# One decoder layer on one core: which queue begins which piece of the first loads

## The chip, the cores and the metric

The kernel runs on 1 NeuronCore of a Trainium2 chip. The metric is the device time of one execution in microseconds (us), as the median over runs; lower is better.

## The reference, cut to what matters

One layer of a decoder trunk on x of shape (1, 256, 1024) in float32: parallel token mixing (two attention branches that share one input projection), cross-attention into 256 memory tokens, a squared-ReLU MLP, and a last RMSNorm. The change touches only the first products, those of the normed input with the first columns of w_in:

```
h = rmsnorm(x, g_mix[l])
proj = h @ w_in[l]
qa = split_heads(proj[..., 0:MOBA_WIDTH], MOBA_HEADS)
```

The kernel multiplies x by the gain g_mix first and applies the row's rsqrt to the products later, so that the products can begin before the norm is known.

## The kernel before

All weights (some 76 MB) are streamed once from HBM in chunks of 128 partitions x 2048 float32 (1 MB). A float32 product is made of three products of halves: each operand is split into a high part (ScalarE, ACT: a copy that rounds to fp32r) and a low part (VectorE, DVE: the whole minus the high part), and TensorE (PE) adds high x high, low x high and high x low in PSUM.

**The head.** The first two chunks of w_in (chunk 0 and chunk 1, 256 output columns each) and the transposed x are not loaded as whole chunks but in nine pieces that lie one behind the other in the tensor `front`, in tile `head_all`. The contraction of 1024 has eight k-tiles of 128 rows:

- piece 0: x and chunk 0 for k-tile 0, and the gains (128 rows of 2176 bytes, 272 KB)
- piece 1: x and chunk 0 for k-tile 1 (128 rows of 2048 bytes, 256 KB)
- piece 2, the pair: chunk 1 for k-tiles 0 and 1 (256 KB)
- pieces 3 to 8, the triples: x, chunk 0 and chunk 1 for k-tiles 2 to 7 (128 rows of 3072 bytes, 384 KB each)

Behind them come four halves (512 KB each) of chunks 2 and 3, the two tiles of x by tokens (`res`), and whole chunks from 4 on.

**Who issues the loads.** Two engines' queues issue transfers: SyncE (SP) and ScalarE (ACT). The tuple `ACT_PIECES` names the pieces that ScalarE begins (line 469); all other pieces, the halves and everything after are SyncE's, in the order of their numbers (lines 346 to 361). Before the change ScalarE begins pieces 1 and 3, and then loads its table of functions (line 470, `preload_act_table_set`).

**What consumes them.** The order is written out by hand and is the same on the three engines: k-tile 0, k-tile 1, the pair, then k-tiles 2 to 7. For each k-tile ScalarE waits for the piece (`head_arrived`), makes `hT_hi` (line 494) and the high part of the weights (line 497; line 502 for the pair); VectorE makes `hT_lo` (line 761) and `w_lo` (line 732); TensorE does its products (line 1226 and its neighbours in `head_products`): 6 matmuls of 256 columns for k-tile 0, 6 for k-tile 1, 12 for the pair, 12 for each triple. Before all of that TensorE runs eight products of zeros (`WARM_UP`, line 1217), which the trace shows as 16 matmuls. Each engine works through its list in order. After the head TensorE goes on with chunks 2, 3, 4 ... (line 1168); a chunk's buffer is loaded again when TensorE has used it (`w_used`), so that later loads follow TensorE.

Of the kernel before, what the change touches and what calls it, by code (L numbers as in the profile page):

```python
# [57 lines left out]
def hybrid_layer(nc, x, front, mem, memT, g_final, weights, ff, out):  # L58
# [66 lines left out]
    FRONT = [2 * SEQ + GAINS, 2 * SEQ, 2 * SEQ] + (KT - FIRST) * [3 * SEQ] + 4 * [CH // 2]  # L125


    ACT_PIECES = (1, 3)

    def front_piece(j):  # L130

        begin = P * sum(FRONT[:j])
        return front[begin:begin + P * FRONT[j]].rearrange("(p n) -> p n", p=P)
# [3 lines left out]
    with ctx:  # L137
# [98 lines left out]
        def piece(j):  # L236

            ends = HEAD - 2 * SEQ * min(j, PAIR + 1) - 3 * SEQ * max(j - PAIR - 1, 0)
            return head_all[:, ends - (2 if j <= PAIR else 3) * SEQ:ends]
# [98 lines left out]
        def _(sp):  # L338
# [7 lines left out]
            for j in range(HEAD_PIECES):  # L346
                dst = piece(j) if j else head_all[:, HEAD - 2 * SEQ:HEAD + GAINS]
                if j not in ACT_PIECES:
                    sp.dma_start(dst, front_piece(j)).then_inc(head_arrived[j], 16)
# [115 lines left out]
        def _(act):  # L465
            copy = nc.scalar.activation

            for j in ACT_PIECES:
                act.dma_start(piece(j), front_piece(j)).then_inc(head_arrived[j], 16)
            nc.scalar.preload_act_table_set("natural_log_exp_and_others")  # L470

            def split_hi(slot, rslot, arrived, used):
                act.wait_ge(raw_in[rslot], arrived)
# [668 lines left out]
        def _(pe):  # L1142
# [77 lines left out]
            def head_products(tiles, n, last=False):  # L1220

                def products(wt, v, wait=None):
                    for c, k in tiles:
                        for m in range(2):
                            a = k * SEQ + m * P
                            i = mm(halves(c)[m], wt[:, c, a:a + P], v[:, k, :],  # L1226
                                   start=k == 0 and m == 0 and wt is w_hi and v is hT_hi,
                                   stop=last and wt is w_lo, skip_group_check=True)
                        if last and wt is w_lo:
                            i.then_inc(w_used, 1)  # L1230

                x_tiles = 1 + max(k for _, k in tiles)
                pe.wait_ge(hi_done[X], x_tiles)
                pe.wait_ge(*((w_hi_ready, 2) if last else (piece_hi, n)))
                products(w_hi, hT_hi)
                pe.wait_ge(lo_done[X], x_tiles)
                products(w_hi, hT_lo)
                pe.wait_ge(*((w_lo_ready, 2) if last else (piece_lo, n)))
                products(w_lo, hT_hi)
# [325 lines left out]
```

## Time and profile before

| what | value |
|---|---|
| median of 3 runs | 412.04 us (411.45 to 412.25) |
| the profiled execution | 412.37 us, span 410.5 us |
| PE busy | 401.8 us (98%) |
| DVE busy | 331.0 us (81%) |
| ACT busy | 251.2 us (61%) |
| HBM traffic | 188 GB/s over the span |

The span runs from the first to the last instruction; the rest of an execution's time lies outside it. All starts below are in us from the span's start. TensorE is busy for nearly the whole span, so what matters is when its work begins, whether it waits afterwards, and what comes after its last product.

### The profile page before, as it was taken

How to read it: one execution, taken by the hardware profiler on the slowest of the kernel's cores; microseconds unless marked ns; L12 is line 12 of the kernel's file. 1: busy time of each engine (PE TensorE's matmuls, PEld its weight loads, DVE VectorE, ACT ScalarE, POOL GpSimd, SP SyncE). 2: the span in 40 equal slices, each digit the busy share in tenths (PEclk: the TensorE clock that was granted, in tenths of full speed). 3: DMA queues.
4: the chain of work that ended last, by engine and by line, in shares of the span. 5: the costliest groups of instructions: out<-in, count | busy, mean ns of one | idle time of the engine just before them, and what ended most of it. 6: DMA issues, size and time to landing. Idle time of an engine off the chain costs nothing.

```text
span 410.5 us, 7028 instructions
## 1 busy us (share of the span) xinstructions
PE 401.8 (98%) x2857; PEld 370.5 (90%) x2857; DVE 331.0 (81%) x410; ACT 251.2 (61%) x298; POOL 27.8 (7%) x41
## 2 busy tenths in 40 slices
PE   8999999999999999999999999999999999999993
PEld 8999978999999999889998899899999999999982
DVE  5769566967755737874958888999999999999985
ACT  7664338864765634561556648777777777777764
POOL 0089000000000000000200000000000000000013
PEclk9999999999999999999999999999999999999998
DMA  8999554534325255545454245455565555656002
GB/s 318 415 419 388 204 204 156 179 126 158 115 102 195 104 206 205 195 184 174 165 170 139 102 145 196 179 208 205 214 203 212 200 206 198 208 206 243 2 0 102
DMA packets 12395, 77.46 MB, mean 189 GB/s; under 512 B 1361, under 2 KB 1361, under 8 KB 4049
## 3 DMA queue, kind: packets, MB, share of 16 engines
q1 hardware_dynamic: 12080, 76.44, 50.6%
q10 hardware_dynamic: 288, 0.66, 0.4%
q8 instruction: 19, 0.31, 0.3%
q14 instruction: 8, 0.06, 0.0%
HBM read 76.04 MB, written 1.05 MB: 188 GB/s over the span
## 4 chain that ended last, share of the span: by engine, by line
PE 91%; DVE 3%; ACT 2%; issue 1%; DMA 1%; POOLq 0%; POOL 0%; DVEq 0%; ACTq 0%
PE bank L1168 36%; PE bank L1496 16%; PE bank L1193 16%; PE bank L1315 11%; PE bank L1226 3%; PE bank L1327 1%; PE bank L1513 1%; PE bank L1420 1%; DMA head_all<-in_front_dram 1%; PE bank L1440 1%; PE bank L1209 1%; PE bank L1368 1%; ACT hT_hi L484 1%; DVE w_lo L732 1%; DVE t_lo L732 1%
## 5 line engine op out<-in xcount | busy, mean ns | idle before, releaser
L732 DVE TENSOR_TENSOR w_lo<-raw,w_hi 128x2048 fp32r<-128x2048 f32 (+2 forms) x69 | 143.6, 2088 | 23.4 <-ACT w_hi L476 22.4
L1168 PE MATMUL bank<-hT_hi,w_hi 128*128 128x256 f32 (+1 forms) x369 | 102.2, 277 | 0.0
L1168 PE MATMUL bank<-hT_lo,w_hi 128*128 128x256 f32 x368 | 101.8, 277 | 0.0
L1168 PE MATMUL bank<-hT_hi,w_lo 128*128 128x256 f32 x368 | 101.7, 276 | 0.0
L476 ACT ACTIVATE w_hi<-raw 128x2048 fp32r<-128x2048 f32 x32 | 61.0, 1917 | 27.4 <-PE bank L1168 14.2
L1168 PEld LDWEIGHTS bank<-hT_hi,w_hi 128*128 128x128 f32 x369 | 69.3, 188 | 0.1
L1168 PEld LDWEIGHTS bank<-hT_lo,w_hi 128*128 128x128 f32 x368 | 69.2, 188 | 0.1
L1168 PEld LDWEIGHTS bank<-hT_hi,w_lo 128*128 128x128 f32 x368 | 69.1, 188 | 0.0
L1315 PE MATMUL bank<-hT_hi,w_hi 128*128 128x256 f32 x128 | 35.8, 279 | 0.0
L1315 PE MATMUL bank<-hT_lo,w_hi 128*128 128x256 f32 x128 | 35.4, 277 | 0.0
L1315 PE MATMUL bank<-hT_hi,w_lo 128*128 128x256 f32 x128 | 35.4, 277 | 0.0
L732 DVE TENSOR_TENSOR t_lo<-t_sum,t_hi 128x2048 fp32r<-128x2048 f32 x15 | 34.4, 2293 | 0.0
L662 ACT ACTIVATE f_hi<-forms 128x896 fp32r<-128x896 f32 (+1 forms) x16 | 15.2, 949 | 27.5 <-DVE forms L1041 26.9
L628 ACT ACTIVATE w_hi<-raw 128x2048 fp32r<-128x2048 f32 x16 | 30.3, 1903 | 0.0
L635 ACT ACTIVATE w_hi<-raw 128x1536 fp32r<-128x1536 f32 (+1 forms) x16 | 24.0, 1500 | 1.4 <-PE bank L1193 1.4
L1315 PEld LDWEIGHTS bank<-hT_hi,w_hi 128*128 128x128 f32 x128 | 24.1, 188 | 0.2 <-issue 0.2
L1315 PEld LDWEIGHTS bank<-hT_lo,w_hi 128*128 128x128 f32 x128 | 24.1, 188 | 0.1
L1315 PEld LDWEIGHTS bank<-hT_hi,w_lo 128*128 128x128 f32 x128 | 24.0, 188 | 0.0
L1496 PE MATMUL bank<-t_lo,f_hi 128*128 128x512 f32 x60 | 23.4, 390 | 0.0
L1496 PE MATMUL bank<-t_hi,f_hi 128*128 128x512 f32 x60 | 23.4, 389 | 0.0
L1496 PE MATMUL bank<-t_hi,f_lo 128*128 128x512 f32 x60 | 23.3, 389 | 0.0
L647 ACT ACTIVATE t_hi<-t_sum 128x1024 fp32r<-128x1024 f32 x15 | 15.9, 1061 | 9.7 <-DVE t_sum L981 9.7
(213 smaller groups left out, 875.0 us busy)
## 6 DMA issues: line engine op xcount, KB each, us to landing
raw<-in_weights_dram SPq DMA_DIRECT2D x64, 1024.0 KB, 4.8
raw<-in_front_dram SPq DMA_DIRECT2D x4, 512.0 KB, 9.2
head_all<-in_front_dram SPq DMA_DIRECT2D x5, 384.0 KB, 6.3
res<-in_x_dram SPq DMA_DIRECT2D x2, 512.0 KB, 12.9
mem_tok<-in_mem_dram SPq DMA_DIRECT2D x1, 1024.0 KB, 11.9
memT_raw<-in_memT_dram SPq DMA_DIRECT2D x1, 1024.0 KB, 10.8
gfin<-in_g_final_dram SPq DMA_DIRECT2D x1, 512.0 KB, 5.5
out_dram<-xs SPq DMA_DIRECT2D x2, 256.0 KB, 2.0
```

Of the source, the lines that this page charges most:

```text
L476: copy(w_hi[:, slot, :], raw[:, rslot, :], ACT.Copy).then_inc(w_hi_ready, 1)
L484: copy(dst[:, k, :], t_tile(n, k), ACT.Copy, scale=gT[:, g + k:g + k + 1]).then_inc(hi_done[n], 1)
L628: copy(w_hi[:, c % RING, :], raw[:, c % RAW, :], ACT.Copy).then_inc(up_hi, 1)
L635: copy(w_hi[:, c % RING, 0:cols], raw[:, c % RAW, 0:cols], ACT.Copy).then_inc(down_hi, 1)
L647: copy(t_hi[:, u % 2, 2 * H:4 * H], t_sum[:, u % 2, 2 * H:4 * H], ACT.Copy).then_inc(t24_hi, 1)
L662: copy(f_hi[:, u % 2, first:upto * P], forms[:, first:upto * P], ACT.Copy).then_inc(f_hi_done, 1)
L732: return nc.vector.tensor_tensor(dst, whole, high.bitcast(fp32), sub)
L1168: last = mm(outs[m][:, tok], w, v[:, k0 + k, tok], start=first and n == 0 and not t, stop=k == nk - 1 and n == 2, skip_group_check=bool(kt ...
L1193: last = mm(outs[t][c][:, a:e], s, w[:, a_ + a:a_ + e], start=start and k == 0 and n == 0, stop=stop and k == nk - 1 and n == 2, skip_grou ...
L1226: i = mm(halves(c)[m], wt[:, c, a:a + P], v[:, k, :], start=k == 0 and m == 0 and wt is w_hi and v is hT_hi, stop=last and wt is w_lo, ski ...
L1315: last = mm(halves(h % 2)[m], w, v[:, kk, :], start=kk == 0 and n == 0, stop=kk == KT - 1 and n == 2)
L1496: last = mm(bank[p][:, a:e], s, w[:, n * H + a:n * H + e], start=start and j == 0, stop=u == PAIRS - 2 and p in (P1, P6, P7) and j == 2, s ...
```

## The change

ScalarE loads its table first and then begins pieces 3, 5 and 7 (the triples of k-tiles 2, 4 and 6). SyncE begins pieces 0, 1, 2, 4, 6 and 8, and then, as before, the halves and the rest. What is loaded, where it goes, and what waits for it stay as they are.

```diff
-    ACT_PIECES = (1, 3)
+    ACT_PIECES = (3, 5, 7)
...
+            nc.scalar.preload_act_table_set("natural_log_exp_and_others")
             for j in ACT_PIECES:
                 act.dma_start(piece(j), front_piece(j)).then_inc(head_arrived[j], 16)
-            nc.scalar.preload_act_table_set("natural_log_exp_and_others")
```

## Rows read from the trace of the kernel before

**Rows 1.** Chain that ended last, in order of time (start, us, what).

```profile
0.73 0.07 issue
0.80 3.50 DMA head_all<-in_front_dram
4.30 0.02 issue
4.33 0.51 ACT hT_hi L494
4.84 0.32 ACT w_hi L497
5.15 0.14 issue
5.29 11.99 PE bank L1226 x96
...
398.17 5.48 PE bank L1513 x24
```

**Rows 2.** Waits of PE over the whole span (us in total, times, longest).

```profile
PE bank L1226 <- ACT w_hi L497: 0.4, 1, 0.4
PE bank L1496 <- DVE f_lo L732: 0.4, 1, 0.4
```

**Rows 3.** DMA issues of 1.1 to 1.3 and of the last head piece (issue to landing).

```profile
head_all<-in_front_dram ACTq DMA_DIRECT2D x1, 384.0 KB, 4.7
head_all<-in_front_dram SPq DMA_DIRECT2D x1, 272.0 KB, 3.5
head_all<-in_front_dram ACTq DMA_DIRECT2D x1, 256.0 KB, 3.7
head_all<-in_front_dram SPq DMA_DIRECT2D x1, 256.0 KB, 4.4
...
head_all<-in_front_dram SPq DMA_DIRECT2D x1, 384.0 KB, 7.2
```

**Rows 4.** Timeline of ACT's queue and engine, 0 to 7 (start, us).

```profile
0.80 0.89 ACTq L469 DMA_DIRECT2D head_all<-in_front_dram  x2
1.72 1.28 ACT L470 ACT_TABLE_LOAD   x1 [1.72 <-PEq L1555]
5.75 0.62 ACT L502 ACTIVATE w_hi<-head_all 128x512 fp32r<-128x512 f32 x1
6.28 0.49 ACT L494 ACTIVATE hT_hi<-head_all 128x256 fp32r<-128x256 f32 x1
6.67 0.62 ACT L497 ACTIVATE w_hi<-head_all 128x512 fp32r<-128x512 f32 x1
```

**Rows 5.** Timeline of PE, 1 to 9.

```profile
1.12 3.78 PE L1217 MATMUL bank<-zeros 128*128 128x128 f32 x16 [1.12 <-DVE zeros L785]
5.85 0.63 PE L1226 MATMUL bank<-hT_lo,w_hi 128*128 128x256 f32 x2
6.28 0.63 PE L1226 MATMUL bank<-hT_hi,w_lo 128*128 128x256 f32 x2
6.71 0.58 PE L1226 MATMUL bank<-hT_hi,w_hi 128*128 128x256 f32 x2
7.13 0.40 PE L1226 MATMUL bank<-hT_lo,w_hi 128*128 128x256 f32 x2
7.59 0.62 PE L1226 MATMUL bank<-hT_hi,w_hi 128*128 128x256 f32 x4
8.95 0.62 PE L1226 MATMUL bank<-hT_hi,w_hi 128*128 128x256 f32 x4
```

**Rows 6.** Packets by DMA queue, 2.5 to 3.5 (q1 is SyncE's, q10 ScalarE's).

```profile
q1 hardware_dynamic: 94, 0.20, 52.0%
q10 hardware_dynamic: 96, 0.19, 49.9%
```

**Rows 7.** Packets by DMA queue, 1.5 to 2, 2 to 2.25 and 2.25 to 2.5.

```profile
q1 hardware_dynamic: 11, 0.02, 41.0%
...
q1 hardware_dynamic: 16, 0.03, 99.4%
q10 hardware_dynamic: 2, 0.00, 4.3%
...
q1 hardware_dynamic: 10, 0.02, 29.9%
q10 hardware_dynamic: 11, 0.02, 26.1%
```

**Rows 8.** Stretch by stretch: busy time of each engine, granted PE clock, DMA share, GB/s.

```profile
3.00:3.25 0.25, 0.25 (x3) 0.25 (x3) 0.00 (x0) 0.01 (x1) 0.00 (x0) 1.00 1.09 405
3.25:3.50 0.25, 0.25 (x3) 0.25 (x3) 0.00 (x0) 0.00 (x0) 0.00 (x0) 1.00 1.02 395
```

**Rows 9.** Timeline of ACT around its second table load.

```profile
138.16 0.58 ACT L525 ACTIVATE aT_hi<-bank 128x512 fp32r<-128x512 f32 x1
138.75 1.28 ACT L578 ACT_TABLE_LOAD   x1
140.05 1.07 ACT L578 ACTIVATE gateT<-gateT 128x1024 f32<-128x1024 f32 x1
```

## The prediction

> **What bounds the kernel now.** I read the chain that ended last first. It begins with the first piece of the head: issued at 0.80, landed at 4.30, then ScalarE's two copies, then TensorE from 5.29 [rows 1]. From there the chain is TensorE almost to the end, and TensorE's own waits say the same: after its start it waits 0.4 us once, for the head, and 0.4 us once, in the MLP [rows 2]. Later loads follow TensorE's use of the buffers, so nothing between 5.29 and the last product at 398.17 is set by a clock of its own. So the time moves by as much as the head's products move, and by nothing else. The question is when each piece of the head lands, and whether TensorE is ready for it.
>
> In the timeline of TensorE the products of k-tile 0 start at 5.29, those of k-tile 1 at 6.71, of the pair at 7.59, of the triple of k-tile 2 at 8.95 [rows 1, 5]. Up to about 7.1 two matmuls of 256 columns take 0.43 us (5.85 to 6.28 to 6.71), 0.213 us each, which is 1.2 GHz; from 7.59 twelve take 1.36 us, 0.113 us each, near 2.4 GHz [rows 5]. The column of the granted clock reads 1.00 in this stretch as well [rows 8], so here the pace is the better witness. By 7.11 TensorE had worked from 1.12 on, with one pause before 5.29.
>
> ScalarE took the copies one behind the other without waiting: the pair's at 5.75, k-tile 2's at 6.28 and 6.67 [rows 4]. A triple costs ScalarE 0.92 us a step (0.39 + 0.53, from the starts), against 1.36 us on TensorE. After the pair TensorE is the slower one, and ScalarE gets ahead of it.
>
> **How the pieces share the DMA engines.** Pieces 0 and 1 were issued together at 0.80 and landed at 4.3 and 4.5; pieces 2 and 3 were issued at 1.24 and landed at 5.64 and 5.94 [rows 3, 4]. Between 2.5 and 3.5 SyncE's queue moved 94 packets and ScalarE's 96 [rows 6]: the two take turns packet by packet, at some 400 GB/s together [rows 8]. A packet is one row of a transfer, 2176 bytes in piece 0, 2048 in pieces 1 and 2, and 3072 in a triple. By 2.5 SyncE's queue had moved 11 + 16 + 10 = 37 packets [rows 7], so that the 91 that were left of piece 0 were through at about 3.5; it landed 0.8 us later. I take 0.8 us from last packet to landing for all.
>
> **The change, part by part.**
>
> *Where ScalarE's transfers begin.* This decides the sign. Either ScalarE's queue issues while the table load runs (issues from about 0.85), or it waits until that is over (from 0.80 + 1.28 = 2.08). No row shows a DMA issue behind a table load. The nearest rows are those of the second table load: it starts 0.01 us after the copy before it ended, and the next activation starts 0.02 us after it [rows 9]. It behaves like a link in the engine's own queue, with the next instruction already handed over, so that whatever hands instructions over did not stand still for the 1.28 us. A DMA issue is the work of that part (it is shown on ACTq, not on ACT, [rows 4]), and I take it that it runs on. The hint is weak, since a table load also starts 0.03 us after a DMA issue [rows 4], which is no longer a gap.
>
> The Trainium skill bears on this (Advanced Engine Details and Errata, Sequencer Loop): an engine instruction is pushed into the engine's queue, and others can be read meanwhile. By that rule the table load holds back no issue, and the sum would be the one below; no run here has shown it yet.
>
> *Piece 0.* Beside it now runs piece 3, with rows of 3072 instead of 2048 bytes. The 91 packets take 91 x (2176 + 3072) bytes = 478 kB, 1.19 us at 400 GB/s instead of 0.96 (91 x 4224): through at 3.7, landed at 4.5, 0.2 us late. TensorE starts 0.99 us after the landing (4.30 to 5.29, [rows 1]): 5.5.
>
> *Piece 1.* It now stands behind piece 0 in SyncE's queue, not beside it. For 128 rows of 2048 bytes beside rows of 3072 the trace has an example: piece 2 beside piece 3, from 3.5 to 5.64 - 0.8 = 4.84, 1.34 us [rows 3]. Strictly packet by packet it would be 128 x 5120 bytes = 655 kB, 1.64 us. I take the measured 1.34, and keep 1.64 as the bound: through at 5.04, landed at 5.84, 1.3 us later than now. Ready for TensorE at 5.84 + 0.99 = 6.83. TensorE is done with k-tile 0 at 5.5 + 1.42 = 6.92, so that this delay is covered, by 0.1 us. (At 1.64 it is 7.13, a wait of 0.2 us, which the next step swallows.)
>
> *Piece 2, the pair.* Another 1.34 us: through at 6.38, landed at 7.18, 1.5 us later than now. ScalarE's copy takes 0.62 us [rows 4], and 0.14 + 0.02 us of handing over [rows 1]: TensorE can start the pair at 7.18 + 0.8 = 7.98. It is done with k-tile 1 at about 7.65 (6 matmuls from 6.92, one or two at the slow pace). It waits 0.3 us, and the pair starts at 7.98 instead of 7.59: **+0.4 us**. With 1.64 us each for pieces 1 and 2: through at 3.7 + 3.28 = 6.98, landed at 7.78, pair at 8.58: +1.0 us.
>
> *The triples.* Pieces 3 and 5 come earlier than they are needed. Piece 4 (k-tile 3) is behind piece 2 in SyncE's queue, beside piece 7: at most 128 x 6144 bytes = 786 kB, 2.0 us: landed at 9.2. ScalarE's two copies (0.39 + 0.62) and the hand-over make 10.35; TensorE needs it at 7.98 + 2 x 1.36 = 10.7. Covered by 0.35 us. The bytes of all the pieces are the same, so the last one still lands at about 3.63 + 7.2 = 10.8 [rows 3] and is needed after 16. Nothing behind it is moved: halves, x and chunks 4 on follow in the same stream of bytes.
>
> *One issue fewer on SyncE, one more on ScalarE.* An issue takes 0.45 us (0.89 for two, [rows 4]). SyncE's list is 0.45 us shorter, which buys nothing: the stream behind the head runs on at full rate and is limited by bytes. ScalarE's three end at 2.2, or at 3.45 if held back; ScalarE idles until 4.3. Nothing else stands in its queue that anyone awaits. The table load itself is hidden before as after; uncovered it would cost 1.28 us.
>
> The sum is +0.4 us, against 412.37 us for the profiled execution and 412.04 us for the median. I put it on the median: **412.4 us**. What a measurement of this kernel can tell from no change is about 0.2%, 0.8 us.
>
> **The rivals.**
>
> *A. The table load holds the issues back.* Then nothing runs beside pieces 0 and 1 (ScalarE's first packets came 1.4 us after its issue, [rows 7]; now at 3.5). By 2.5 between 37 and all 50 packets of both queues are piece 0's; the other 78 to 91, at 2176 bytes each, take 0.42 to 0.50 us: landed at 3.7 to 3.8, TensorE ready at 4.7 to 4.8. The warm-up products cover this: sixteen from 1.12 at 0.22 us each end their turn at 4.7 [rows 5]. TensorE starts 0.5 to 0.6 us early. Piece 1 lands at 4.5 or before; the pair (by 3.65 + 1.64 + 0.8 = 6.1) is ready at 6.9, before TensorE wants it. If the pace still steps up at 7.1, the 2.6 matmuls gained are worth only 0.113 us each, 0.3 us; if it steps with the work, the whole 0.55. Time 411.5 to 411.7. For it: the release of the other queue is plain arithmetic. Against it: rows 9.
>
> Here the Trainium skill has a price of its own (ScalarE: Activation LUTs, What ACT_TABLE_LOAD costs): a drain of about 1.38 us beside the 1.28 us. With both, the issues would begin at about 3.5 and the triple of k-tile 2 would come about 0.1 us after TensorE wants it, an estimate from that page. The trace disagrees: activations start 0.02 us behind the load [rows 9].
>
> *B. The queues take turns strictly.* The end on the slow side: the 1.64 us bound holds for both pieces, and the pair starts at 8.58. Time 413.0. It decides once piece 2 lands later than 7.6 (pair at 8.4). For it: 94 to 96 packets [rows 6]. Against it: piece 2 took 1.34 us in the same company.
>
> *C. The queues share by bytes.* Then piece 0 isn't late, piece 1 is through at 3.5 + 541/400 = 4.85 and the pair's at 4.85 + 1.31 = 6.16, landed at 6.96, pair at 7.76: +0.2 us, 412.2, as good as no change. Against it: rows 6, though there the rows were of nearly one size.
>
> **How the numbers follow.** Forecast 0.47, A 0.28, B 0.15, C 0.10. Medians of three runs here lie 0.8 us apart at most, so I give each case about 0.4 us either way. Slower by over 0.2% (above 412.86): most of B and a tenth of the forecast, 0.17. Faster by over 0.2% (below 411.22): a fifth of A, 0.06. Within: 0.77. The range goes from A's lower end, 411.4, to B's value with a little of its spread, 413.1.
>
> **What the profile after would show.** ScalarE's three issues at about 0.85 to 2.2 (A: 2.1 to 3.45). Piece 0 landed at 4.5, piece 1 at 5.8, piece 2 at 7.2. TensorE's first product at 5.5, a wait of about 0.3 us before the pair's, the pair at 8.0; from there everything 0.4 us later than before, and no other new wait. The prediction is wrong if TensorE's first product comes before 5.2, if a triple is awaited, or if the step of the pace has moved by 1 us or more.

## The result and the profile after

The changed kernel takes **414.26 us** (median of 6 runs, 414.04 to 416.21) against 411.83 us before (median of 6). The ratio is **1.0068, 95% interval 1.0055 to 1.0082**: slower by about 2.4 us of the medians, where +0.4 us and 412.4 us were forecast, too little to be told from no change. It lies above the forecast range, which ended at 413.1 us.

The profiled execution took 414.14 us with a span of 412.2 us, 1.7 us more than the span before. The chain that ended last begins as follows (start, us, what); the rows of before are [rows 1]. The products are counted up to 13 us only.

```profile
0.80 3.94 DMA head_all<-in_front_dram
4.74 0.02 issue
4.76 0.51 ACT hT_hi L494
5.27 0.31 ACT w_hi L497
5.59 0.14 issue
5.72 3.16 PE bank L1226 x12
...
8.88 4.20 PE bank L1226 x32
```

The first piece lands 0.44 us later (4.74 instead of 4.30) and TensorE's first product comes 0.43 us later. The larger step comes behind it: the pair starts at 8.88 instead of 7.59 ([rows 5]). The timeline of ScalarE and its queue shows why, beside [rows 4].

```profile
0.79 1.28 ACT L468 ACT_TABLE_LOAD   x1 [0.79 <-PEq L1555]
0.82 1.36 ACTq L470 DMA_DIRECT2D head_all<-in_front_dram  x3
...
6.30 0.51 ACT L494 ACTIVATE hT_hi<-head_all 128x256 fp32r<-128x256 f32 x1 [0.72 <-DMA head_all<-in_front_dram]
...
8.11 0.63 ACT L502 ACTIVATE w_hi<-head_all 128x512 fp32r<-128x512 f32 x1 [1.00 <-DMA head_all<-in_front_dram]
8.65 0.49 ACT L494 ACTIVATE hT_hi<-head_all 128x256 fp32r<-128x256 f32 x1
```

The three issues begin at 0.82, while the table load runs from 0.79 to 2.07: it holds nothing back. ScalarE, which before went from copy to copy, now waits for piece 1 (until 6.3) and for the pair (until 8.1). SyncE issues pieces 0, 1 and 2 at 0.80, 1.24 and 1.71. The lines of the DMA issues give their landings (last column, us from issue to landing).

```profile
head_all<-in_front_dram ACTq DMA_DIRECT2D x1, 384.0 KB, 4.2
head_all<-in_front_dram SPq DMA_DIRECT2D x1, 272.0 KB, 3.9
...
head_all<-in_front_dram SPq DMA_DIRECT2D x1, 256.0 KB, 5.0
...
head_all<-in_front_dram SPq DMA_DIRECT2D x1, 256.0 KB, 6.4
```

Piece 0: 0.80 + 3.9 = 4.7. Piece 1: 1.24 + 5.0 = 6.2. Piece 2: 1.71 + 6.4 = 8.1, against 5.64 before [rows 3]. The timeline of TensorE around it:

```profile
7.82 0.63 PE L1226 MATMUL bank<-hT_lo,w_hi 128*128 128x256 f32 x2
8.25 0.63 PE L1226 MATMUL bank<-hT_hi,w_lo 128*128 128x256 f32 x2
8.88 1.02 PE L1226 MATMUL bank<-hT_hi,w_hi 128*128 128x256 f32 x4
9.74 0.62 PE L1226 MATMUL bank<-hT_lo,w_hi 128*128 128x256 f32 x4
```

In this execution the pace stays at 0.21 us a product up to about 9.5 (before: 7.1, [rows 5]), so that the pair's first four products take 0.86 us instead of 0.45. The 1.29 us at the pair become 1.70 us behind it, and 1.70 us is the difference of the spans. From k-tile 2 on this trace is that of before, shifted.

### The profile page after: what moved, and what is told of

Same layout as the page of the kernel before. It is cut to its first block, busy times and chain, and to the rows that moved or that the text cites. A ratio compares the mean times of both kernels' runs of the same rounds, so it can differ in the third digit from the quotient of the medians.

```text
span 412.2 us, 7028 instructions
## 1 busy us (share of the span) xinstructions
PE 403.0 (98%) x2857; PEld 371.3 (90%) x2857; DVE 330.5 (80%) x410; ACT 250.8 (61%) x298; POOL 28.0 (7%) x41
## 4 chain that ended last, share of the span: by engine, by line
PE 91%; DVE 3%; ACT 2%; issue 1%; DMA 1%; POOLq 0%; POOL 0%; DVEq 0%; ACTq 0%
PE bank L1168 36%; PE bank L1496 16%; PE bank L1193 16%; PE bank L1315 11%; PE bank L1226 3%; PE bank L1327 1%; PE bank L1513 1%; DMA head_all<-in_front_dram 1%; PE bank L1420 1%; PE bank L1440 1%; PE bank L1209 1%; PE bank L1368 1%; ACT hT_hi L484 1%; DVE t_lo L732 1%; DVE w_lo L732 1%
```

## The experiments

Each kernel was timed against the kernel before in the same rounds. The ratio is to that kernel, with its 95% interval. The start of the pair and the landing of piece 2 are from one profiled execution each (us).

| run | ScalarE's pieces | ratio (95%) | piece 2 lands | pair starts |
|---|---|---|---|---|
| before | 1, 3 | 1 | 5.6 | 7.6 |
| changed | 3, 5, 7 behind the table load | 1.0068 (1.0055 to 1.0082) | 8.1 | 8.9 |
| pieces_only | 3, 5, 7 ahead of it | 1.0055 (1.0041 to 1.0069) | 8.0 | 8.8 |
| table_only | 1, 3 behind it | 1.0008 (0.9996 to 1.0020) | 5.7 | 7.5 |
| sp_only | none | 1.0011 (1.0000 to 1.0022) | 5.3 | 6.3 |
| act1 | 1 | 1.0009 (0.9998 to 1.0019) | 5.2 | 7.0 |
| act12 | 1, 2 | 1.0007 (0.9990 to 1.0023) | 5.8 | 7.5 |
| act3 | 3 | 1.0040 (1.0025 to 1.0054) | 6.2 | 7.4 |
| act35 | 3, 5 | 1.0050 (1.0033 to 1.0067) | 7.3 | 8.7 |
| held | 3, 5, 7 after the table load is over | 1.0053 (1.0038 to 1.0067) | 7.6 (again: 5.4) | 8.4 (again: 6.8) |

**The two parts of the change, each alone.** First the split of the pieces without the move of the table load:

```diff
-    ACT_PIECES = (1, 3)
+    ACT_PIECES = (3, 5, 7)
```

> The changed kernel with the table load put back behind ScalarE's three issues, so that only the split of the pieces differs from before. Theory 1 (the triples in ScalarE's queue take three fifths of the bytes while pieces 0, 1 and 2 wait, and the table load has no part in it): as slow as the changed kernel, ratio 1.005 to 1.008; piece 2 lands at about 8.1 and the pair starts at 8.7 to 9.0. Theory 2 (the table load beside the first issues slows the first packets: 143 GB/s at 2.5 to 2.75 against 364 before): the first packets come as fast as before, piece 2 lands at about 7.2, ratio 1.001 to 1.003.

Then the move without the split (`ACT_PIECES = (1, 3)`, table load ahead of the issues):

```diff
+            nc.scalar.preload_act_table_set("natural_log_exp_and_others")
             for j in ACT_PIECES:
                 act.dma_start(piece(j), front_piece(j)).then_inc(head_arrived[j], 16)
-            nc.scalar.preload_act_table_set("natural_log_exp_and_others")
```

> The kernel before with its own pieces 1 and 3 in ScalarE's queue, but with the table load ahead of the issues. Theory 1: no change (0.998 to 1.002); piece 0 lands at 4.3 and the pair starts at 7.6. Theory 2: pieces 0 to 2 land 0.3 us or more later than before and the rate at 2.5 to 2.75 is near 143 GB/s; ratio 1.001 to 1.003.

The split alone gives the whole loss (1.0055, the interval overlaps that of the changed kernel), the move alone none (1.0008, interval across 1). Theory 2 falls: in table_only the rate at 2.5 to 2.75 was 298 GB/s (364 and 407 in the two profiles of before) and piece 0 landed at 4.0, earlier than in the first profile of before, while in pieces_only the rate was 209 GB/s with the table load out of the way. The slow first packets go with the triples; whether the table load takes a little of the rate too isn't shown, and it costs no time that can be told.

**What runs beside pieces 0 to 2: a ladder.** Only the tuple `ACT_PIECES` differs, and the table load stands behind the issues: `()`, `(1,)`, `(3,)`, `(3, 5)` and `(1, 2)`.

> The kernel before with all nine pieces in SyncE's queue, in the order of their numbers. Theory 1 (only what runs beside pieces 0 to 2 delays them): piece 0 lands at 3.7, piece 1 at 4.4, piece 2 at 5.1, all before TensorE wants them; TensorE starts at 4.7 instead of 5.3; ratio 0.9985 to 1.000. Theory 4 (one queue alone cannot keep the 16 DMA engines full in the first microseconds, as in the run with held issues, where piece 2 took 3.2 us from piece 1): piece 2 lands after 6.5 and the ratio is above 1.002.

> Only piece 1 in ScalarE's queue. Pieces 0 and 1 land as before (4.3 and 4.5) by every theory. Theory 1: piece 2 has the engines to itself and lands at 5.1 instead of 5.64; no gain, since TensorE wants it at 7.6: ratio 0.999 to 1.001. Theory 4: piece 2 lands after 6.0; ratio 1.000 to 1.002.

> Only piece 3 in ScalarE's queue, pieces 0, 1, 2 and all later ones in SyncE's. Theory 1: piece 3 runs beside pieces 0 and 1 alone, so that these land about as in the changed kernel (4.5 to 4.7 and 5.8 to 6.2), but piece 2 has the engines to itself and lands at about 6.7 instead of 8.1; the pair starts near 7.6, ratio 1.000 to 1.002. Theory 5 (the mere order, pieces 1 and 2 behind piece 0 in one queue, costs what the changed kernel lost): piece 2 at about 8, ratio above 1.004.

> Pieces 3 and 5 in ScalarE's queue, the others in SyncE's: the step between one triple (ratio 1.004) and three (1.0055 to 1.0068). Theory 1 (what delays pieces 0 to 2 is the bytes that run beside them): two triples are 256 packets, and SyncE's pieces 0 to 2 are 384, so piece 2 is left alone for its last third or so and lands between the 6.3 or less of one triple and the 8.0 of three, at about 7.4; ratio 1.004 to 1.006. Theory 5 (order alone): piece 2 lands at 8.0 as with three.

> Pieces 1 and 2 in ScalarE's queue, 0 and all triples in SyncE's: the order of landings of before with the roles turned for pieces 2 and 3. Theory 1: piece 0 beside piece 1 as before (4.0 to 4.3), piece 2 beside piece 3, packet for packet, lands at 5.6 to 6.0, in time for the pair at 7.0 to 7.6; ratio 0.999 to 1.001. Rival (ScalarE's queue gives its pieces later than SyncE's whatever they are, since its first packets come 0.5 us later): pieces 1 and 2 late by 0.5 us, still in time, ratio up to 1.002.

With no, one, two and three triples in ScalarE's queue piece 2 lands at 5.3, 6.2, 7.3 and 8.0 (pieces_only): about 0.9 us for each triple. It stands in the same place of SyncE's queue in all four, so theory 5, the order alone, falls, and theory 1 holds for the landings. Theory 4 isn't borne out by sp_only either: piece 2 landed at 5.3, not after 6.5. The timeline of ScalarE shows the start of the pair's copy, one line each from sp_only, act3 and act35 (in the first two it follows right behind the copy before it, so that it shows only the latest that the piece can have landed):

```profile
5.37 0.63 ACT L502 ACTIVATE w_hi<-head_all 128x512 fp32r<-128x512 f32 x1
```

```profile
6.33 0.62 ACT L502 ACTIVATE w_hi<-head_all 128x512 fp32r<-128x512 f32 x1
```

```profile
7.33 0.63 ACT L502 ACTIVATE w_hi<-head_all 128x512 fp32r<-128x512 f32 x1
```

The landings of piece 2 don't account for the times of act3 and act35. In act3 the pair starts at 7.43, between the two starts of before (7.03 and 7.59), and still the median of its twelve executions is 413.75 us (412.17 to 414.99); the profiled one took 413.08, and what the longer ones do is not shown. In act35 the pair's copy starts at 7.33, so that the pair was ready at about 8.1. But TensorE had waited 1.2 us before its first product and 0.6 us before k-tile 1, and its clock fell back: from 8.0 to 11.0 the granted clock (the third column from the right) is 0.50, the level of 1.2 GHz.

```profile
7.50:8.00 0.50, 0.50 (x3) 0.50 (x4) 0.47 (x3) 0.50 (x2) 0.00 (x0) 0.79 0.97 393
8.00:8.50 0.50, 0.50 (x5) 0.50 (x4) 0.50 (x1) 0.50 (x2) 0.00 (x0) 0.50 1.00 399
```

So the pair started at 8.65, behind slow products, and its own twelve took 2.56 us instead of 1.36.

act12, which turns the roles for pieces 2 and 3, is as good as before: rows of 2048 and 3072 bytes side by side are no loss in themselves, as long as the pieces wanted first are begun first in both queues. act3 was dearer (1.004) than the "1.000 to 1.002" that went with theory 1: there the time was missed, though piece 2 landed even earlier (6.2) than the 6.7 expected. In its profile piece 0 lands at 4.8, TensorE's first product comes at 5.79, 0.5 to 0.8 us late, and from the pair on the products run at 0.1178 us each (below).

Taking everything away from beside piece 0 gains nothing. In sp_only piece 0 lands at 3.5 and the pair starts at 6.3, but TensorE then waits at k-tile 2 and k-tile 2 starts at 8.18. These are the waits of its TensorE:

```profile
PE bank L1217 <- DVE zeros L785: 1.1, 1, 1.1
PE bank L1496 <- DVE f_lo L732: 0.4, 1, 0.4
PE bank L1226 <- ACT w_hi L497: 0.3, 1, 0.3
```

**The issues truly held.** A one-column copy behind the table load, and a wait for it, make what rival A supposed:

```diff
+        table_done = sem("table_done")
...
             nc.scalar.preload_act_table_set("natural_log_exp_and_others")
+            act.wait_ge(half_ready, 1)
+            copy(mo_rsum[:, 0:1], half[:, 0:1], ACT.Copy).then_inc(table_done, 1)
+            act.wait_ge(table_done, 1)
             for j in ACT_PIECES:
```

> The changed kernel with ScalarE's issues truly held until its table load is over, by a one-column copy behind the load and a wait on it; issues from about 2.3 instead of 0.82. Theory 1: pieces 0 and 1 run alone, piece 0 lands at 3.7 to 3.8 and piece 1 by 4.5; the pair starts before 7.6; ratio 0.998 to 1.000, so 0.005 or more below the changed kernel. Rival (what costs is the mere number of bytes ahead in two queues or the order of the copies, not when the triples start): ratio above 1.003.

> The kernel with issues held until the table load is over, once more. In its first profile pieces 0 and 1 landed early (3.7 and 4.4), but the rate fell to 154 to 283 GB/s between 3.5 and 6.5 and piece 2 landed at 7.6. If that fall belongs to the kernel (a second queue that begins while the first is under way, or SyncE's queue alone), it is there again and piece 2 lands after 6.5; if it was a chance of that execution, piece 2 lands at 5.0 to 6.0.

The landings of pieces 0 and 1 are those forecast for rival A (3.7 and 4.3), and TensorE starts at 4.69. Still the ratio is 1.0053, not the 0.998 to 1.000 expected by theory 1. In the second execution the pair is in time (6.8), but the triple of k-tile 2, issued at 2.32, takes 6.6 us to land at 8.9. The DMA issue and TensorE's waits of held_again:

```profile
head_all<-in_front_dram ACTq DMA_DIRECT2D x1, 384.0 KB, 6.6
```

```profile
PE bank L1230 <- ACT w_hi L501: 1.8, 1, 1.8
```

The rate is low meanwhile (GB/s, last column of the stretches of held_again):

```profile
4.00:4.50 0.50, 0.50 (x5) 0.50 (x3) 0.14 (x1) 0.50 (x3) 0.00 (x0) 1.00 1.41 326
4.50:5.00 0.50, 0.50 (x3) 0.45 (x3) 0.50 (x2) 0.50 (x3) 0.00 (x0) 1.00 0.75 229
5.00:5.50 0.50, 0.50 (x4) 0.50 (x4) 0.50 (x3) 0.32 (x2) 0.00 (x0) 1.00 1.10 283
```

In the first execution it fell to 154 to 283 GB/s between 3.5 and 6.5, and there it was piece 2 that came late (7.6). TensorE then waited 1.8 us for the pair, and the granted clock was 0.50 from 9.0 to 12.0, so that part of that execution's time is the clock's. So a low rate belongs to this kernel, and which piece it hits varies. act1 has such a stretch as well (219 and 199 GB/s between 4 and 5), sp_only a weaker one, and act3 one from 5.5 on, when ScalarE's triple is over (264 GB/s from 5.5 to 6). SyncE's queue alone is not enough to explain it: in before it ran alone from 5.5 to 6.5 at about 400 GB/s. Why was not found out.

**TensorE's pace.** The changed kernel with 11 warm-up products (`WARM_UP = 11`), and both kernels once more:

> The changed kernel with 11 warm-up products of zeros instead of 8 (22 matmuls at 0.22 us, ending near 6.0 in place of 4.7, so k-tile 0 starts at about 6.0 instead of 5.72, in time behind piece 2). Theory 3 (TensorE's pause of 0.8 us before its first product is why the pace steps up at 9.55 instead of 7.11): the step is back near 7.1, the pair's twelve products take 1.36 us instead of 1.77, and the ratio is about 0.001 (0.4 us) below the changed kernel's. Rival (the time of the step varies from execution to execution whatever the kernel does): no change against the changed kernel in the mean, and the step somewhere between 7 and 10.5.

> The kernel before once more, for what differs from execution to execution: when the pace of TensorE steps up (7.11 in the first profile; if it varies whatever the kernel does, it will lie elsewhere, between 4 and 10.5), and the landings of pieces 0 to 3 (4.3, 4.5, 5.6, 5.9 within 0.3 us, if they are set by the kernel).

> The changed kernel once more, for what differs from execution to execution. If the landings are the kernel's: piece 0 at 4.5 to 4.8, piece 2 at 7.9 to 8.2, the pair at 8.7 to 8.9; the step of the pace may lie anywhere between 4 and 10.5.

after_warm11: ratio 1.0067 (1.0053 to 1.0081), no gain. Its pace stepped up at about 4.2, before its warm-up differed at all from that of the changed kernel, whose two executions stepped at 9.5 and 6.2; those of before stepped at 7.1 and 6.2. So the time of the step varies from execution to execution and is no mark of either kernel. The landings repeat: before 4.3, 4.5, 5.6 and again 4.0, 4.2, 5.4; changed 4.7, 6.2, 8.1 and again 4.4, 6.0, 7.8.

base_again and after_again stepped at nearly one time (6.21 and 6.24), so they are the pair to set side by side. All starts in us:

| mark | before, again | changed, again | later by |
|---|---|---|---|
| first product | 4.99 | 5.41 | 0.42 |
| pair | 7.03 | 8.60 | 1.57 |
| k-tile 2 | 8.39 | 10.09 | 1.70 |
| the 87 products of chunks 2 and 3 | 16.71 | 18.73 | 2.02 |
| chunk 3's end and on (202 products) | 27.00 | 29.41 | 2.41 |
| span | 409.9 | 412.3 | 2.4 |

The spans differ by the 2.4 us of the medians (the times of these two executions, 411.99 and 414.69, by 2.7). 1.57 us are the late pair. The other 0.84 us arise behind it, without a wait. Two lines of the chain in order of time show it, first those of base_again, then of after_again:

```profile
16.71 9.86 PE bank L1168 x87
27.00 22.90 PE bank L1168 x202
```

```profile
18.73 10.25 PE bank L1168 x87
29.41 22.91 PE bank L1168 x202
```

The 87 products take 0.39 us more: 0.1178 instead of 0.1133 us each. The same pace holds from the pair on. It ends where two things stand together in the kernel: the lone product of line 1256 and, right behind it, a product of line 1168 that is done in two halves of 128 columns. In table_only, which has the slower pace too:

```profile
27.67 0.59 PE L1256 MATMUL bank<-rstd_diag,neg_ones_r 128*128 128x256 f32 x2
27.91 0.52 PE L1168 MATMUL bank<-hT_hi,w_hi 128*128 128x128 f32 x2
```

Which of the two ends it there can't be told.

**Is the slower pace the price of a wait?** Spare copies on ScalarE (three in late3, six in late6 and late6_halved) make k-tile 3 late by other means, and in late6_halved and after_halved one product is done in two halves of 128 columns:

```diff
             for k in range(FIRST, KT):
+                if k == 3:
+                    for spare in ([v_tok[:, t, a:a + 512] for t in range(2) for a in (0, 512)]
+                                  + [flat(qkT[:, a:a + 2, :]) for a in (8, 10)])[:6]:
+                        copy(spare, piece(PAIR), ACT.Copy)
                 head_high(k)
...
-                            i = mm(halves(c)[m], wt[:, c, a:a + P], v[:, k, :],
-                                   start=k == 0 and m == 0 and wt is w_hi and v is hT_hi,
-                                   stop=last and wt is w_lo, skip_group_check=True)
+                            split = (c, k, m) == (0, 4, 0) and wt is w_hi and v is hT_hi
+                            for tok in ((slice(0, P), slice(P, SEQ)) if split else (slice(0, SEQ),)):
+                                i = mm(halves(c)[m][:, tok], wt[:, c, a:a + P], v[:, k, tok],
+                                       start=k == 0 and m == 0 and wt is w_hi and v is hT_hi,
+                                       stop=last and wt is w_lo, skip_group_check=True)
```

> The kernel before with three spare copies of 512 columns on ScalarE ahead of k-tile 3 (3 x 0.53 = 1.6 us; their results are used by nothing). k-tile 3 is then ready at about 9.9, when TensorE wants it at 9.75 to 10.3: a control. Both theories: no wait or one under 0.2 us, ratio 0.999 to 1.001.

> The same with six spare copies (3.2 us): k-tile 3 is ready at about 11.5, so that TensorE, which mostly has its full pace by then, waits 1.2 to 1.7 us. Theory 6 (after a wait at the full pace the products run on at 0.1175 us each instead of 0.113 until the lone product of line 1256, some 160 products later): the end moves by the wait and 0.7 us more, 1.9 to 2.4 us, ratio 1.0046 to 1.0058, and the stretch of 87 products on line 1168 takes 10.25 us. Rival (the two paces are a chance of the execution): the wait alone, 1.2 to 1.7 us, ratio 1.003 to 1.004, and the stretch may show either.

> The six spare copies, and one product of k-tile 4 (the first, high x high of chunk 0) done as two of 128 columns. The kernel already does this at two places behind waits. Theory 6: the pace is back at 0.113 behind it; the stretch on line 1168 takes 9.86 us and the ratio is 0.0012 to 0.0017 below that of the six copies alone. Rival: no difference.

> The changed kernel with the same product of k-tile 4 in two halves. Theory 6: most of its executions lose about 0.7 us to the slower pace behind the waits of the pair; that comes back: ratio 1.004 to 1.005 instead of 1.0055 to 1.0068, and the stretch on line 1168 takes 9.86 us. Rival: ratio 1.0055 to 1.007 as before.

late3: 1.0013 (1.0003 to 1.0022), above the "0.999 to 1.001" expected of it, with a wait of 0.2 us and the slow pace (10.25 us for the 87). late6: 1.0073 (1.0051 to 1.0095), dearer than either theory expected (1.0046 to 1.0058, and 1.003 to 1.004). But its profiled execution, the fastest of its six (413.29 us), waits 0.9 us at the full pace and goes on at 0.113 all the same:

```profile
11.16 0.71 PE L1230 MATMUL bank<-hT_hi,w_hi 128*128 128x256 f32 x4 [0.94 <-ACT w_hi L497]
11.71 0.62 PE L1230 MATMUL bank<-hT_lo,w_hi 128*128 128x256 f32 x4
12.17 0.62 PE L1230 MATMUL bank<-hT_hi,w_lo 128*128 128x256 f32 x4
```

So theory 6 falls in its strict form: a wait doesn't always bring the slower pace. after_halved shows the same: it waits 0.6 and 0.8 us at the full pace, and from 9.32 on, long before its halved product at 12.95, four products take 0.45 us. In late6_halved the slow pace was there before the wait, and the halved product ended it, as the timeline shows (four products in 0.47 us ahead of it, in 0.45 behind it):

```profile
12.04 0.63 PE L1232 MATMUL bank<-hT_lo,w_hi 128*128 128x256 f32 x4
12.51 0.63 PE L1232 MATMUL bank<-hT_hi,w_lo 128*128 128x256 f32 x4
12.98 0.73 PE L1232 MATMUL bank<-hT_hi,w_hi 128*128 128x128 f32 x5
13.55 0.62 PE L1232 MATMUL bank<-hT_lo,w_hi 128*128 128x256 f32 x4
14.00 0.62 PE L1232 MATMUL bank<-hT_hi,w_lo 128*128 128x256 f32 x4
```

The timings are too close to count what it is worth: late6_halved 1.0057 (1.0035 to 1.0079) beside 1.0073, after_halved 1.0059 (1.0046 to 1.0071) beside 1.0068. Both differences have the expected sign and lie inside the intervals. 1.0059 is also what the rival expected (1.0055 to 1.007), and theory 6 expected 1.004 to 1.005; since the profiled execution of after_halved had the full pace anyway, it tests little.

No version beat the kernel before.

## Why the prediction was wrong, point by point

**Where ScalarE's transfers begin: right.** The issues run beside the table load, from 0.82. The step rested on a weak row [rows 9] and a rule of the Trainium skill (Advanced Engine Details and Errata, Sequencer Loop); the trace agrees with that rule. In held, where a copy stands directly behind the load, it starts at 2.08, 0.01 us behind the load's end. The drain of some 1.38 us that the Trainium skill adds (ScalarE: Activation LUTs, What ACT_TABLE_LOAD costs) isn't seen there, and the measurement decides.

**Piece 0: right in kind, short in size.** Forecast landing 4.5, measured 4.7 and 4.4, against 4.3 and 4.0 before: a delay of 0.4 us in both pairs of profiles instead of 0.2.

**Pieces 1 and 2: this step failed, and it made most of the loss.** "I take the measured 1.34, and keep 1.64 as the bound." They took 1.5 and 1.8 us (ScalarE's copies, which waited for them, start at 4.76, 6.30 and 8.11; in the second execution 4.45, 6.05 and 7.82, 1.6 and 1.8 us): piece 2 landed at 8.1 and 7.8 instead of 7.18, and the pair started at 8.9 and 8.6 instead of 7.98. Piece 1 wasn't quite covered either: TensorE waited 0.3 us for it in the second execution. The 1.34 us was the time of one transfer whose neighbour happened to begin late: ScalarE's queue had a pause between two transfers just then (10 packets against SyncE's 40 between 3.75 and 4 in the first profile of before). Such pauses fall on SyncE's queue as well. The two pieces together took 3.4 us in both executions, a little more than the 3.28 us of strict turns, so that 1.64 us was nearly the right price and yet no bound. The packets by DMA queue in the changed kernel from 5.45 to 7.3, the stretch of piece 2 by the same 0.8 us from last packet to landing, show it:

```profile
q10 hardware_dynamic: 172, 0.48, 64.3%
q1 hardware_dynamic: 158, 0.28, 40.0%
```

ScalarE's queue moved 0.48 MB, some 156 rows of a triple, while SyncE's moved the 128 rows of piece 2: more than one for one. Two transfers stood ahead of the pair in SyncE's queue, and around the end of one its turns carry next to nothing. These are the packets of after_again from 3.75 to 4, where piece 0 ends:

```profile
q10 hardware_dynamic: 32, 0.10, 96.8%
q1 hardware_dynamic: 14, 0.00, 5.1%
```

**The rate at the start: not forecast.** "Some 400 GB/s together" was taken as given from 2.5 on. With a triple beside piece 0 it comes later. The same stretches as in [rows 8], here 2.5 to 3.5, in the changed kernel:

```profile
2.50:3.00 0.50, 0.50 (x5) 0.50 (x4) 0.00 (x0) 0.00 (x0) 0.00 (x0) 1.00 0.73 186
3.00:3.50 0.50, 0.50 (x4) 0.50 (x4) 0.00 (x0) 0.00 (x0) 0.00 (x0) 1.00 0.96 312
```

Summed over the stretches from 1.5 to 3.5, the two queues had moved 0.33 to 0.43 MB in the six profiles with a triple first in ScalarE's queue (act3, act35, both of the changed kernel, pieces_only, after_warm11), and 0.48 to 0.55 MB in all of the others that were summed, sp_only and held_again among them. That is up to 0.4 us at 400 GB/s, and it is part of the late landings above, the one of piece 0 above all, not beside them.

**The sum was made against one execution's pace.** "It waits 0.3 us", at the pair, was what was left after k-tile 1's slow products in a profile whose pace stepped up at 7.1. The step comes earlier in other executions. Then the kernel before starts the pair sooner, 7.03 in base_again, while the changed kernel waits for the data whatever the pace: the pair came 1.29 us later in the first two profiles and 1.57 us in the second two. The forecast should have priced the landing against the fastest start that TensorE can make (from 4.99 with 12 products at 0.113 to 0.213 us each, 6.35 to 7.55), not against the one seen.

**"By as much as the head's products move, and by nothing else": too strong.** Of the 2.4 us of the second pair of profiles, 0.84 came behind the pair, from the slower pace of the products up to line 1256. Whether the slower pace follows from the waits is open: nine profiles have the slower pace in these 87 products, and in eight of them (after_again, after_warm11, sp_only, act1, act3, held, held_again, late3) TensorE waited for ScalarE in the head. But of the nine that have the full pace there, seven waited in the head too (before, changed, pieces_only, act35, late6, after_halved, and late6_halved, whose pace is full only from its halved product on), and table_only has the slower pace with no wait.

Term by term the 2.4 us are the 0.4 forecast (7.98 - 7.59), 0.6 for the later landing (8.60 - 7.98), 0.6 for the earlier start that the kernel before can make (7.59 - 7.03), and the 0.8 of the pace.

**The rivals.** B was nearest: it put the start of the pair at 8.58, and it was 8.9 and 8.6. Its 413.0 us were still short by 1.2 us, because it too was counted from the one execution's start of the pair (7.59), and because it left out the pace. A's premise is refuted by the issues at 0.82, and A's result by held: with the premise granted, the late triple of k-tile 2 eats the gain. The working of A looked only at whether the pair came in time. C would have had pieces 1 and 2 through in 1.35 and 1.31 us (its 541 kB should be the 524 of the second term, which changes 0.04 us); they took 1.5 to 1.8, so it falls too.

**The triples: right.** Behind the pair no product waited for a piece in either profile of the changed kernel.

## What to carry to other kernels

Where two queues feed a chain that takes pieces in a fixed order, a piece's landing is set by everything that either queue has begun before it: put the first-wanted pieces first in both queues. Price a transfer that runs beside others from the total moved until it ends, with the ends of the transfers ahead of it counted against it; one neighbouring transfer's duration is not a bound. And price a stall against the fastest the consumer can be there, not against the one execution in the profile.

## What the runs showed of the hardware that was not expected

- DMA issues on ScalarE's queue run during a table load on ScalarE: the load from 0.79 to 2.07, the issues from 0.82.
- The pace of TensorE steps from 0.21 to 0.113 us for 256 columns, from the 1.2 GHz level to near that of 2.4 GHz, at a time that varies by execution: about 4.2, 6.2, 9.5 and 10.2 in four with the same start of the warm-up (after_warm11, after_again, changed, pieces_only). It can also fall back: after 1.8 us without a product in the first held run (granted clock 0.50 from 9.0 to 12.0), and in act35 after waits of 1.2 and 0.6 us (0.50 from 8.0 to 11.0). At the first step the column of the granted clock shows nothing: it reads 1.00 at either pace.
- Products of 256 columns with a weight load each run at 0.1133 or at 0.1178 us. An execution keeps one of them over a hundred and more products. The slower one ended at a product done in halves in late6_halved, and in the nine others at the lone product of line 1256 with a halved one right behind it. What starts it is open.
- With SyncE's queue alone, or ScalarE's joining late, the rate fell to 154 to 344 GB/s for 1 us and more in the first 7 us (sp_only, act1, act3, both of held; in stretches of 0.5 us), where before and act12 held 350 or more from 2.75 on. The cause is open.
